# Three gate tiles moved between the last latent heads, and the queries' rotation split between two heads and two engines

## The chip, the cores and the metric

The kernel runs on one core of a Trainium2 chip. Its five engines are TensorE (PE in the profile; its weight loads are PEld), VectorE (DVE), ScalarE (ACT), GpSimd (POOL) and SyncE (SP, which here only issues DMAs; SPq in the profile). The metric is the device time of one execution in microseconds (us), less being better. The profile shows one execution; its times are us from the start of the span.

## The reference

Two transformer blocks follow each other over 512 positions of width 1024: a pooling layer, a multi-head latent attention layer (MLA), a final norm, then a second block with another attention, a spatial gate and a feed-forward part. The change lies in the MLA layer alone:

```python
h = rmsnorm(x, norm_g)
proj = h @ w_in
q_lat, kv_lat, k_rope, z = ...          # 384, 256, 64 and 2048 columns of proj
q = (rmsnorm(q_lat, q_norm_g) @ w_q_b)  # 16 heads of 128 (q_nope) + 64 (q_rope)
kv = (rmsnorm(kv_lat, kv_norm_g) @ w_kv_b)  # 16 heads of 128 (k_nope) + 128 (v)
q_rope, k_rope = apply_rope(...)        # t1*cos - t2*sin, t2*cos + t1*sin
s = (q_nope @ k_nope + q_rope @ k_rope) * scale, causal mask, softmax, @ v
return x + (o.reshape(B, S, 2048) * silu(z)) @ w_out
```

`z` is the gate: 2048 columns, held as 16 chunks of 128.

## The kernel before

All products are made in three passes: each factor is split into a high and a low part, and `three` adds hi*hi, hi*lo and lo*hi in one PSUM bank (eight banks of 128x512). Weights come as tiles of 128x1024 from one stream in HBM. SyncE loads tile t into one of two buffers `raw`, ScalarE makes its high part `w_hi` (`split_tile`, L497), GpSimd its low part `w_lo` (`low_tiles`, L450), TensorE uses it. A ring of four split tiles lies between; `split_tile` for tile t does the work for tile t+3. The order of work on each engine is written out by hand, and each engine goes strictly by its own order: whatever waits holds all behind it on that engine.

**Projection (`mla_in`).** 22 tiles of eight 128-row chunks: 5 latent chunks, one for the key's rotated part, and 16 for the gate. Each is 24 matmuls (`projection`), scaled by `inv` on VectorE into `z` (L1059) and put through Silu on ScalarE (L628). Its input `mla_xg` is written over later by v, q and the rotated queries.

**Heads.** 16 heads in 4 groups (`GROUPS`) of 4 (`GH`). For a group, five weight tiles give 14 units (`GROUP_TILES`): k, q and v of four heads and two rope halves, each half for all four heads. A unit goes to bank 6 or 7; ScalarE copies its high part (L581), VectorE its low part (L999). A group's units are made one group ahead, between the heads of the group before: after head h, `prepare(g, j)` with g = h // 4 + 1 and j = h % 4. With j = 0 come k0 and both rope halves, with j = 1 k1, q0, q1, with j = 2 k2 and q2, with j = 3 k3, q3 and the four v. After heads 12 to 15 there is nothing of this to do.

One head h on TensorE: transposes of its probabilities (L1504), blocks 0 and 1; scores of head h+1 for blocks 0 and 1; transposes and scores for blocks 2 and 3; the product with v (`weigh_mla`); the units. The scores of a block are three products for q and k, two for the rotated part (L1492, L1493) and one of `ident_r` with `mask_r`, which adds the causal mask (L1494). Per head, ScalarE does the high parts of the transposes (L657), the exponentials (L641) and one normalisation (L649); VectorE their low parts (L1118), the maxima (L1099), the normalisation (L1112) and the gate product (L1142). The second pair of transposes waits until VectorE has the low part of block 0.

**Rotation of the queries.** For a group g >= 1 VectorE turns both halves out of the banks with j = 0 (`turn_half`: 2 operations L1010, L1011 for the first half, 4 for the second, L1013 to L1018). With j = 1 ScalarE makes the high parts (`turn_split`, L602) and VectorE the low parts (`turned_low`, L1023). SyncE then places them into `rope_q`: 8 DMAs for the high parts as soon as both are made, 8 for the low (`rope_rows`, L393). SyncE's order is: weight tiles up to the fifth of group g, the 8 high rows, one weight tile, the 8 low rows, four weight tiles. That one weight tile is the one that ScalarE splits with j = 2. The scores of the group's first head, made within head 4g-1 (j = 3), wait for all 16 (`rope_q_in`).

**End of the heads.** ScalarE makes `y_hi` of the finished gate chunks (L556) in heads 12 to 15, GpSimd `y_lo` (L457, 128x512), and `out_product` ("mla_out") uses chunks 0 to 7 with its first tile and 8 to 15 with its second, waiting for each `y_lo`.

Of the kernel before, what the change touches and what calls it, by code (L numbers as in the profile page):

```python
# [21 lines left out]
P = 128  # L22
S = 512
# [28 lines left out]
EPS = 1e-6  # L52
MASKED = -1e30
# [20 lines left out]
TILE_SIZES = (("pool_u", PC), ("pool_z", PC), ("pool_group", PC * PG // 8), ("pool_out", PC), ("mla_in", LC + 1 + PC + 1),  # L74
              ("heads", 5 * GROUPS - 1), ("mla_out", PC), ("mix_qk", 9), ("mix_v", 4), ("mix_z", 8),
# [19 lines left out]

def unit_place(kind, j):
# [8 lines left out]
EARLY = LC + 1 + PC - 3  # L105
# [29 lines left out]
class NormSemaphores:  # L135

    def __init__(self, sem, stage, before, common):
        self.before = before
        self.mean, self.prepared, self.inv = common
        self.x_ready = sem(f"{stage}_x_ready") if stage != "pool" else None  # L140
        self.xg_hi = sem(f"{stage}_xg_hi")
        self.xg_lo = sem(f"{stage}_xg_lo")
        self.squared = sem(f"{stage}_squared")
        self.summed = sem(f"{stage}_summed")
# [15 lines left out]
def build(nc, x_in, stream, columns, counts_in, positions, rows_in, w_s, spill, out):  # L160
# [5 lines left out]
    with ctx:  # L166
# [73 lines left out]
        rope_q = place(112, "rope_q", [P, 2, GH, S], f32r)  # L240
        prob = place(128, "prob", [P, ROW[NB]])
        prob_t_hi, prob_t_lo = (place(133 + 5 * i, f"prob_t_{i}", [P, COLUMN[NB]], f32r) for i in range(2))
        turned_1, turned_2 = place(72, "turned_1", [P, S]), place(74, "turned_2", [P, S])
        rope_t = place(143, "rope_t", [P, S])
# [37 lines left out]
        def col(name, k=0):  # L282
# [11 lines left out]
        common = sem("norm_mean"), sem("norm_prepared"), sem("norm_inv")  # L294
        norm = {n: NormSemaphores(sem, n, before, common)
                for n, before in (("pool", 0), ("mla", 1), ("mix", 2), ("ffn", 4))}
# [18 lines left out]
        x_spilled, x_back = sem("x_spilled"), sem("x_back")  # L315
        unit_done, unit_hi, unit_evac = sem("unit_done"), sem("unit_hi"), sem("unit_evac")
        turned, turned_hi_done, turned_lo_done, rope_q_in = sem("turned"), sem("turned_hi_done"), sem("turned_lo_done"), sem("rope_q_in")

# [39 lines left out]

        def hi_units(u):
# [14 lines left out]
        def _(sp):  # L374
# [20 lines left out]

            for turn, j in sweep(sp, TILE["heads"]):
                load(turn, j)
            for i in range(5 * GROUPS):
# [21 lines left out]
            for turn, j in sweep(sp, TILE["mix_z"] + 3, first=TILE["heads"] + 5 * GROUPS):  # L420
# [15 lines left out]
        def _(pool):  # L436
# [16 lines left out]
            low_tiles(TILE["mla_out"] + RING)  # L453

            for k in range(PC):
# [1391 lines left out]
```

## Time and profile before

| | us |
|---|---|
| median of 3 runs | 1398.18 |
| lowest, highest | 1396.94, 1398.90 |
| the profiled execution | 1397.49 |
| its span | 1395.8 |
| TensorE busy within the span | 1341.2 |

Heads 0 to 15 take from 484.5 to 681.1 us of the span. Projections before and products behind them run with TensorE busy throughout. An idle time in brackets in the timeline is the engine's own, ahead of the row, with what released it; "issue" time has no releaser in the profile. A row's time is from its start to its modelled end, and rows of TensorE overlap.

### The profile page before, as it was taken

What the parts mean: (1) busy time and instruction counts of PE and PEld (TensorE: products, weight loads), DVE (VectorE), ACT (ScalarE), POOL (GpSimd) and SP (SyncE); (2) the same over time, 40 slices, a digit from 0 to 9 for tenths busy, and PEclk for the clock granted to TensorE, in tenths of its full rate; (3) what the DMA queues carried; (4) which work ended last, traced back from release to release, by engine and by line L of the source; (5) the groups of instructions that cost most, each with busy time, mean ns of one, the idle gap of its engine ahead of it and who ended that gap; (6) DMA issues with size and microseconds to landing.
All of it is one profiled execution on the core that took longest, in us unless ns stands there. A gap on an engine that the chain in (4) does not pass through costs nothing.

```text
span 1395.8 us, 16836 instructions
## 1 busy us (share of the span) xinstructions
PE 1341.2 (96%) x6234; PEld 1095.4 (78%) x6234; DVE 656.9 (47%) x1015; ACT 537.9 (39%) x893; POOL 552.2 (40%) x247
## 2 busy tenths in 40 slices
PE   7999999999999999999899999988989999999997
PEld 5888888887788787887788778876768888888886
DVE  7998647133643466666334764466652222221001
ACT  5234333223332555656433335655333223222112
POOL 4446444444353412213544343152344444443441
PEclk9999999999999999999999999999999999999999
DMA  4233222324132421322232336422222223222221
GB/s 153 89 105 119 100 93 91 103 91 151 62 120 78 133 61 46 94 57 77 79 102 91 106 141 177 115 65 95 90 91 90 90 90 97 98 90 91 91 100 67
DMA packets 40589, 135.44 MB, mean 97 GB/s; under 512 B 5937, under 2 KB 5937, under 8 KB 40017
## 3 DMA queue, kind: packets, MB, share of 16 engines
q1 hardware_dynamic: 38800, 126.18, 28.3%
q10 hardware_dynamic: 1728, 8.44, 1.6%
q8 instruction: 40, 0.66, 0.2%
q14 instruction: 21, 0.16, 0.0%
HBM read 117.76 MB, written 6.29 MB: 89 GB/s over the span
## 4 chain that ended last, share of the span: by engine, by line
PE 86%; DVE 5%; ACT 3%; issue 3%; POOL 1%; DMA 1%; SPq 0%; DVEq 0%; ACTq 0%; POOLq 0%
PE bank L1364 27%; PE bank L1366 27%; PE bank L1365 27%; PE bank L1504 2%; PE bank L1492 1%; PE bank L1493 1%; DVE pool_xg L869 1%; ACT f_prob L641 1%; POOL w_lo L450 1%; PE bank L1388 0%; DVE ffn_xg L869 0%; DMA x<-x_in 0%; DVE pool_sqsum L879 0%; ACT w_hi L497 0%; DVE prob_t L1118 0%
## 5 line engine op out<-in xcount | busy, mean ns | idle before, releaser
L450 POOL TENSOR_TENSOR w_lo<-raw,w_hi 128x1024 fp32r<-128x1024 f32 x209 | 513.1, 2456 | 780.1 <-ACT w_hi L497 780.1
L497 ACT ACTIVATE w_hi<-raw 128x1024 fp32r<-128x1024 f32 x209 | 220.2, 1054 | 424.6 <-PE bank L1366 376.9
L1364 PE MATMUL bank<-ffn_xg,w_hi 128*128 128x512 f32 x352 | 140.1, 398 | 5.1 <-DVE ffn_xg L869 5.1
L1366 PE MATMUL bank<-ffn_xg,w_lo 128*128 128x512 f32 x352 | 139.4, 396 | 0.0
L1365 PE MATMUL bank<-ffn_xg,w_hi 128*128 128x512 f32 x352 | 139.4, 396 | 0.0
L1364 PE MATMUL bank<-pool_xg,w_hi 128*128 128x512 f32 x256 | 102.7, 401 | 9.5 <-DVE pool_xg L869 9.5
L1365 PE MATMUL bank<-pool_xg,w_hi 128*128 128x512 f32 x256 | 102.2, 399 | 0.0
L1366 PE MATMUL bank<-pool_xg,w_lo 128*128 128x512 f32 x256 | 102.2, 399 | 0.0
L1364 PE MATMUL bank<-y_hi,w_hi 128*128 128x512 f32 x256 | 101.3, 396 | 0.0
L1366 PE MATMUL bank<-y_hi,w_lo 128*128 128x512 f32 x256 | 101.2, 396 | 0.0
L1365 PE MATMUL bank<-y_lo,w_hi 128*128 128x512 f32 x256 | 101.2, 395 | 0.0
L1364 PEld LDWEIGHTS bank<-ffn_xg,w_hi 128*128 128x128 f32 x352 | 66.1, 188 | 22.8 <-DVE ffn_xg L869 6.6
L1366 PEld LDWEIGHTS bank<-ffn_xg,w_lo 128*128 128x128 f32 x352 | 66.3, 188 | 16.5
L1365 PEld LDWEIGHTS bank<-ffn_xg,w_hi 128*128 128x128 f32 x352 | 66.3, 188 | 16.4 <-issue 0.2
L894 DVE TENSOR_TENSOR x<-bank,x 128x512 f32<-128x512 f32 x16 | 11.1, 692 | 127.8 <-PE bank L1366 127.8
L1364 PE MATMUL bank<-mla_xg,w_hi 128*128 128x512 f32 x176 | 70.2, 399 | 0.0
L1365 PE MATMUL bank<-mla_xg,w_hi 128*128 128x512 f32 x176 | 69.4, 394 | 0.0
L1366 PE MATMUL bank<-mla_xg,w_lo 128*128 128x512 f32 x176 | 69.4, 394 | 0.0
L1366 PE MATMUL bank<-w_hi,act 128*128 128x512 f32 x176 | 69.4, 394 | 0.0
L1364 PE MATMUL bank<-w_hi,act 128*128 128x512 f32 x176 | 69.0, 392 | 0.0
L1365 PE MATMUL bank<-w_lo,act 128*128 128x512 f32 x176 | 69.0, 392 | 0.0
L1364 PEld LDWEIGHTS bank<-pool_xg,w_hi 128*128 128x128 f32 x256 | 48.8, 191 | 21.4 <-POOL w_lo L450 9.5
(333 smaller groups left out, 2845.9 us busy)
## 6 DMA issues: line engine op xcount, KB each, us to landing
raw<-stream SPq DMA_DIRECT2D x209, 512.0 KB, 3.4
spill<-x ACTq DMA_DIRECT2D x2, 2048.0 KB, 6.8
rope_q<-turned_hl SPq DMA_DIRECT2D x64, 64.0 KB, 2.2
stacked<-fq SPq DMA_DIRECT2D x24, 128.0 KB
stacked<-fk SPq DMA_DIRECT2D x24, 128.0 KB
x<-x_in SPq DMA_DIRECT2D x4, 512.0 KB, 6.9
x<-spill ACTq DMA_DIRECT2D x1, 2048.0 KB, 7.7
x<-spill SPq DMA_DIRECT2D x1, 2048.0 KB, 7.8
```

Source lines behind the costliest of these rows:

```text
L450: pool.tensor_tensor(w_lo[:, j % RING, :], raw[:, j % RAW, :], plain(w_hi[:, j % RING, :]), ALU.subtract).then_inc(tile_lo, 1)
L497: act.activation(w_hi[:, t % RING, :], raw[:, t % RAW, :], ACT.Copy).then_inc(tile_hi, 1)
L641: act.activation(target[:, ROW[b]:ROW[b + 1]], bank[SCORE_BANK[b]][:, SCORE_AT[b]:SCORE_AT[b] + n], ACT.Exp, bias=neg_peak[:, h % 2, b:b + ...
L869: dve.scalar_tensor_tensor(xg_lo[:, k, :], x[:, k, :], gain(k), plain(xg_hi[:, k, :]), ALU.mult, ALU.subtract).then_inc(n.xg_lo, 1)
L894: dve.tensor_tensor(x[:, k, :], bank[(k + 4) % 8][:], x[:, k, :], ALU.add).then_inc(n.x_ready, 1)
L1364: pe.matmul(target, a_hi, b_hi, start=start, stop=False)
L1365: pe.matmul(target, a_hi, b_lo, start=False, stop=False)
L1366: return pe.matmul(target, a_lo, b_hi, start=False, stop=stop)
L1492: pe.matmul(target, rope_q[:, g % 2, j, a], rope_k_hi[:, 0:n], start=False, stop=False)
L1493: pe.matmul(target, rope_q[:, g % 2, j, a], rope_k_lo[:, 0:n], start=False, stop=False)
L1504: last = pe.transpose(bank[3 + b % 2][:, P * (q - b):P * (q - b + 1)], source[:, ROW[q] + P * b:ROW[q] + P * (b + 1)], ident[:])
```

## The change

It has three parts. The causal mask as a product on TensorE stands in both kernels alike (L1494 before).

1. **Gate tiles.** The last three gate chunks (`ZN = PC - 3`) leave the projection and get three tiles of their own (`mla_late`) behind the heads' tiles. TensorE makes them after heads 12, 13 and 14 (`late_gate`), in banks 6 and 7, 24 matmuls each. Since their input would be gone, ScalarE stores both parts of `mla_xg` to HBM after the first projection tile (two DMAs of 2 MB), and SyncE reloads them (7 of 8 chunks in three DMAs once group 3's rows are placed, the last chunk after head 11's units). VectorE scales each product, and ScalarE puts it through Silu one head later, with an Exp of one column behind it in head 13.
2. **Rotation.** With j = 0 VectorE turns the first half only; ScalarE copies the second half out of its bank into `rope_2`. VectorE turns it with j = 2, between the normalisation and the gate product. High parts, low parts: with j = 2 instead of j = 1. SyncE's order around the rows is the same.
3. **Order of `y_hi` and `y_lo`.** `y_hi` of chunks 8 and 9 moves from head 14 to head 15. GpSimd takes the four first tiles of `mla_out` between the `y_lo` rather than ahead of them.

```diff
+ZN = PC - 3
+ZX_PARTS = ((108, 3), (143, 3), (72, 1), (64, 1))
...
 sync
+            load(0, TILE["heads"] + 5 * GROUPS)
+            sp.wait_ge(mla.scores, 3 * 12)
+            sp.wait_ge(zx_spilled, 32)
+            sp.wait_ge(rope_q_in, 256 * GROUPS)
+            for i in range(3):
+                reload(i)
+            load(0, TILE["heads"] + 5 * GROUPS + 1)
+            sp.wait_ge(tile_used, group_tile(GROUPS - 1, GH) + 1)
+            reload(3)
...
 gpsimd
-            low_tiles(TILE["mla_out"] + RING)
-            for k in range(PC):
-                pool.wait_ge(y_hi_done, PC + k + 1)
-                pool.tensor_tensor(y_lo[:, k, :], ...)
+            low_tiles(TILE["mla_out"] + 1)
+            first = TILE["mla_out"] + 1
+            for n, chunks in enumerate((range(0, 4), range(4, 8), range(8, 10), range(10, PC))):
+                if n:
+                    low_tiles(first + 1, first=first)
+                    first += 1
+                for k in chunks:
+                    pool.wait_ge(y_hi_done, PC + k + 1)
+                    pool.tensor_tensor(y_lo[:, k, :], ...)
...
 scalar, prepare_tile
+                    elif by_scalar((kind, g, k)):
+                        wait_unit(act, (kind, g, k))
+                        if g > 1:
+                            act.wait_ge(turned, 2 * g)
+                        act.activation(rope_2[:], bank[...][:], ACT.Copy).then_inc(rope_copied, 1)
 scalar, projection
+                if u == 1:
+                    act.wait_ge(norm["mla"].xg_lo, norm["mla"].chunks + DC)
+                    for i, part in enumerate((mla_xg_hi, mla_xg_lo)):
+                        act.dma_start(xg_spill[:, :, i, :], plain(part[:])).then_inc(zx_spilled, 16)
 scalar, heads
                 if g < GROUPS:
-                    if j == 1:
+                    if j == 2:
                         turn_split(g)
                     prepare(g, j)
-                elif h == 12:
+                elif h < HEADS - 1:
+                    split_tile("mla_late", 0, h - 12)
+                else:
                     split_tile("mla_out", 0, 0)
-
-                for k in {12: range(0, 4), 13: range(4, 8), 14: (8, 9), 15: range(10, 14)}.get(h, ()):
+                if h > 12:
+                    n = h - 13 + ZN
+                    act.wait_ge(mla_evac, LC + 1 + n + 1)
+                    act.activation(z[:, n, :], z[:, n, :], ACT.Silu).then_inc(mz_silu, 1)
+                    if h + 2 < HEADS:
+                        settle(act.activation(inv_sum[:, h % 2, 0:1], ones[:, 0:1], ACT.Exp))
+                for k in {12: range(0, 4), 13: range(4, 8), 15: range(8, 14)}.get(h, ()):
                     y_high(k, PC)
...
 vector, heads
+                if j == 0:
+                    unit_low(("k", g, 0))
+                    turn_half(g, 0)
+                    return
...
+                if g < GROUPS and j == 2:
+                    turn_half(g, 1)
                 dve.wait_ge(mla.weighted, h + 1)
                 dve.wait_ge(mz_silu, h + 1)
                 dve.tensor_tensor(z[:, h, :], bank[5][:], z[:, h, :], ALU.mult).then_inc(mla.out, 1)
                 if g < GROUPS:
-                    if j == 1:
+                    prepare(g, j)
+                    if j == 2:
                         turned_low(g)
-                    prepare(g, j)
+                elif h < HEADS - 1:
+                    n = h - 12
+                    dve.wait_ge(tile_used, TILE["mla_late"] + n + 1)
+                    dve.tensor_tensor(z[:, ZN + n, :], bank[6 + n % 2][:], inv[:], ALU.mult).then_inc(mla_evac, 1)
...
 tensor
+            def late_gate(n):
+                wait_tile(0, t)
+                pe.wait_ge(zx_back, 16 * len(ZX_PARTS))
+                ...
+                for k in range(DC):
+                    i, c = ZX_AT[k]
+                    last = three(bank[6 + n % 2][:], *wblock(t, k), zx[i][:, c, 0, :], zx[i][:, c, 1, :], k == 0, k == DC - 1)
...
                 weigh_mla(h)
                 if g < GROUPS:
                     prepare(g, j)
+                elif h < HEADS - 1:
+                    late_gate(h - 12)
```

On ScalarE, this stood between heads 1 and 2 before (`turned_hl`: the high parts of the turned queries; `w_hi`: the split of a weight tile; `prob_t`: the transposes' high parts):

```order
L649 ACTIVATE prob<-prob,inv_sum 128x512
L602 ACTIVATE turned_hl<-turned 128x512 x2
L581 ACTIVATE k<-bank 128x512
L497 ACTIVATE w_hi<-raw 128x1024
L581 ACTIVATE q<-bank 128x512 x2
```

and this stands between heads 2 and 3 now:

```order
L692 ACTIVATE prob<-prob,inv_sum 128x512
L641 ACTIVATE turned_hl<-turned 128x512 x2
L615 ACTIVATE k<-bank 128x512
L530 ACTIVATE w_hi<-raw 128x1024
L615 ACTIVATE q<-bank 128x512
L700 ACTIVATE prob_t<-bank 128x512
```

The pair `turned_hl` moved by one head; the tile split behind it is now that of j = 2.

On SyncE, waits shown, group 1's rows stood and stand alike; this is the kernel after, from the fifth tile of group 1 on:

```order
L398 DMA raw<-stream 128x1024 [waits tile_lo] x5
L409 DMA rope_q<-turned_hl 32x512 [waits turned_hi_done]
L409 DMA rope_q<-turned_hl 32x512 x7
L398 DMA raw<-stream 128x1024 [waits tile_lo]
L409 DMA rope_q<-turned_hl 32x512 [waits turned_lo_done]
L409 DMA rope_q<-turned_hl 32x512 x7
L398 DMA raw<-stream 128x1024 [waits tile_lo] x4
```

Nothing moved here; the two waits now refer to work that stands a head later.

On VectorE the end of head 2 reads now (before, only the last `TENSOR_SCALAR`, `z`, `k` and `q` of these stood there):

```order
L1171 TENSOR_SCALAR prob<-prob,inv_sum 128x384
L1068 TENSOR_TENSOR rope_t<-rope,sin 128x512
L1069 TENSOR_TENSOR turned<-turned,rope_t 128x512
L1071 TENSOR_TENSOR rope_t<-rope,cos 128x512
L1077 TENSOR_TENSOR turned<-turned,rope_t 128x512
L1207 TENSOR_TENSOR z<-bank,z 128x512
L1050 TENSOR_TENSOR k<-bank,k 128x512
L1050 TENSOR_TENSOR q<-bank,q 128x512
L1082 TENSOR_TENSOR turned_hl<-turned,turned_hl 128x512 x2
L1177 TENSOR_TENSOR prob_t<-bank,prob_t 128x512
```

Four operations moved here from the end of head 0, and the two low parts (L1082) from head 1.

## Rows read from the trace of the kernel before

**Rows 1.** The page: busy time, share of the span, instructions.

```profile
PE 1341.2 (96%) x6234; PEld 1095.4 (78%) x6234; DVE 656.9 (47%) x1015; ACT 537.9 (39%) x893; POOL 552.2 (40%) x247
```

**Rows 2.** Waits of TensorE, whole span: us in total, times, longest.

```profile
PE bank L1504 <- DVE prob_t L1118: 8.7, 6, 1.8
```

**Rows 3.** Timeline of VectorE, heads 0 to 2: start, duration, what [idle before].

```profile
497.27 0.69 DVE L1013 TENSOR_TENSOR rope_t<-bank,sin 128x512 f32<-128x512 f32 x1 [0.68 <-PE bank L1366]
...
499.44 0.69 DVE L1018 TENSOR_TENSOR turned<-turned,rope_t 128x512 f32<-128x512 f32 x1
500.06 1.15 DVE L1118 TENSOR_TENSOR prob_t<-bank,prob_t 128x512 fp32r<-128x512 f32 x2
...
507.17 1.28 DVE L1023 TENSOR_TENSOR turned_hl<-turned,turned_hl 128x512 fp32r<-128x512 f32 x2
...
518.47 0.88 DVE L1112 TENSOR_SCALAR prob<-prob,inv_sum 128x128 f32<-128x128 f32 x3
```

**Rows 4.** Timeline of TensorE, heads 0, 1 and 3.

```profile
484.50 0.93 PE L1504 MATMUL bank<-ident,prob 128*128 128x128 f32 x7
...
491.43 0.44 PE L1364 MATMUL bank<-lat,w_hi 128*128 128x512 f32 x1
...
500.89 0.70 PE L1504 MATMUL bank<-ident,prob 128*128 128x128 f32 x3 [1.57 <-DVE prob_t L1118]
...
522.47 0.30 PE L1364 MATMUL bank<-k,q 128*128 128x128 f32 x1
```

**Rows 5.** Timeline of ScalarE, heads 0 to 2.

```profile
491.65 0.72 ACT L649 ACTIVATE prob<-prob,inv_sum 128x512 f32<-128x512 f32 x1 [0.24 <-DVE inv_sum L1109]
...
506.40 1.14 ACT L602 ACTIVATE turned_hl<-turned 128x512 fp32r<-128x512 f32 x2
...
520.38 1.05 ACT L497 ACTIVATE w_hi<-raw 128x1024 fp32r<-128x1024 f32 x1
```

**Rows 6.** SyncE's timeline, group 1: issue start, duration of the series, count.

```profile
507.56 4.95 SPq L393 DMA_DIRECT2D rope_q<-turned_hl  x8
512.55 0.58 SPq L382 DMA_DIRECT2D raw<-stream  x1
513.17 4.94 SPq L393 DMA_DIRECT2D rope_q<-turned_hl  x8
```

**Rows 7.** Landing after issue: tile turned_hl; then line L382, 505 to 530 us.

```profile
DMA to landing us min/median/max: 1.9/2.2/3.8
...
DMA to landing us min/median/max: 3.4/3.7/4.6
```

**Rows 8.** Busy time by window: us, busy (instructions) by engine, clock, DMA share, GB/s.

```profile
345.00:445.00 100.00, 100.00 (x425) 79.24 (x424) 44.49 (x43) 33.51 (x44) 43.10 (x18) 1.00 0.28 90
```

**Rows 9.** Timeline of TensorE, heads 12 to 15.

```profile
647.60 0.93 PE L1504 MATMUL bank<-ident,prob 128*128 128x128 f32 x7
...
676.46 0.98 PE L1504 MATMUL bank<-ident,prob 128*128 128x128 f32 x7 [1.32 <-DVE prob L1112]
...
681.09 0.44 PE L1364 MATMUL bank<-y_hi,w_hi 128*128 128x512 f32 x1
```

**Rows 10.** Timeline of ScalarE: a table load at 120 us, and head 13.

```profile
120.81 1.28 ACT L549 ACT_TABLE_LOAD   x1
122.11 0.63 ACT L549 ACTIVATE z<-z 128x512 f32<-128x512 f32 x1
...
666.78 2.18 ACT L556 ACTIVATE y_hi<-z 128x512 fp32r<-128x512 f32 x4
```

**Rows 11.** Timeline of GpSimd, head 15.

```profile
680.29 7.55 POOL L457 TENSOR_TENSOR y_lo<-z,y_hi 128x512 fp32r<-128x512 f32 x6 [0.95 <-ACT y_hi L556]
```

**Rows 12.** Timeline of TensorE, the first tile: half clock, then full.

```profile
9.51 0.77 PE L1364 MATMUL bank<-pool_xg,w_hi 128*128 128x512 f32 x1 [9.51 <-DVE pool_xg L869]
...
14.77 0.42 PE L1364 MATMUL bank<-pool_xg,w_hi 128*128 128x512 f32 x1
```

**Rows 13.** Landing of the 2 MB transfers (tensor spill), us after issue.

```profile
DMA to landing us min/median/max: 6.3/7.5/7.8
```

More of the change, by code:

```diff
@@ L93 @@
 CHUNKS_OF = {"k": KC, "q": QC, "rope": QC}
+ZX_PARTS = ((108, 3), (143, 3), (72, 1), (64, 1))
+ZX_AT = [(i, c) for i, (_, n) in enumerate(ZX_PARTS) for c in range(n)]
 def unit_place(kind, j):
@@ L240, in build @@
         rope_q = place(112, "rope_q", [P, 2, GH, S], f32r)
+        zx = [place(at, f"zx_{i}", [P, n, 2, S], f32r) for i, (at, n) in enumerate(ZX_PARTS)]
         prob = place(128, "prob", [P, ROW[NB]])
@@ L357, in wait_unit, with by_scalar, evacuated @@
                 engine.wait_ge(unit_done, sum(not ends_tile(o) for o in UNITS[:UNIT[u] + 1]))
+        def by_scalar(u):
+            return u[0] == "rope" and u[1] > 0 and u[2] == 1
+        def evacuated(u):
+            return sum(not by_scalar(o) for o in UNITS[:UNIT[u] + 1])
         def hi_units(u):
@@ L418, in stack_head @@
                     sp.dma_start(slot[at:at + 2, which, :], plain(c_parts[h:h + 1, part:part + 2, :])).then_inc(head_stacked[h % 2], 16)
-            for turn, j in sweep(sp, TILE["mix_z"] + 3, first=TILE["heads"] + 5 * GROUPS):
+            for turn, j in sweep(sp, TILE["mix_z"] + 3, first=TILE["heads"] + 5 * GROUPS + 2):
                 load(turn, j)
@@ L605, in _ @@
             act.dma_start(spill, x[:]).then_inc(x_spilled, 16)
-            for u in range(LC + 1 + PC):
+            for u in range(LC + 1 + ZN):
                 if u == EARLY:
@@ L1030, in prepare_tile @@
                         unit_low((kind, g, k))
-            for u in range(LC + 1 + PC):
+            for u in range(LC + 1 + ZN):
                 if u == EARLY:
@@ L1373, in wait_tile, with projection @@
                 pe.wait_ge(tile_lo, turn * RING + (t + 1))
-            def projection(stage, turn, j, b, xg_hi, xg_lo, xg_lo_done=None):
+            def projection(stage, turn, j, b, xg_hi, xg_lo, first=None):
                 t = TILE[stage] + j
@@ L1379, in projection @@
                 for k in range(DC):
-                    if xg_lo_done is not None:
-                        pe.wait_ge(xg_lo_done, k + 1)
+                    if first is not None:
+                        pe.wait_ge(first.xg_lo, first.chunks + k + 1)
                     last = three(b[:], *wblock(t, k), xg_hi[:, k, :], xg_lo[:, k, :], k == 0, k == DC - 1)
@@ L1406, in _ @@
                     pe.wait_ge(in_evac, turn * RING + (j - 3))
-                projection("pool_u", turn, j, bank[j % 4], pool_xg_hi, pool_xg_lo, n.xg_lo if starts(turn, j, 1) else None)
+                projection("pool_u", turn, j, bank[j % 4], pool_xg_hi, pool_xg_lo, n if starts(turn, j, 1) else None)
                 if starts(turn, j, 2) and j == 1:
@@ L1460, in _ @@
             n = norm["mla"]
-            for u in range(LC + 1 + PC):
+            for u in range(LC + 1 + ZN):
                 if u < 4:
@@ L1704, in _ @@
                     pe.wait_ge(ffn_evac, turn * RING + (j - 3))
-                projection("ffn_up", turn, j, bank[j % 4], ffn_xg_hi, ffn_xg_lo, n.xg_lo if starts(turn, j, 1) else None)
+                projection("ffn_up", turn, j, bank[j % 4], ffn_xg_hi, ffn_xg_lo, n if starts(turn, j, 1) else None)
                 if starts(turn, j, 1):
```

83 lines of the change are left out of this document (52 added, 31 removed).

## The prediction

> **What bounds the kernel now.** I read the page's busy times first: TensorE is busy for 1341.2 of 1395.8 us [rows 1], so it is the bound and all that can be won or lost is its idle time and its half-clock time. Next come TensorE's waits: 8.7 us in six waits for `prob_t`'s low part [rows 2]. The timeline of the heads shows where. At the end of heads 0, 4 and 8 VectorE turns both rope halves, its last operation starts at 499.44, and the low part that TensorE needs follows at 500.06 [rows 3]; TensorE stood still 1.57 us for it at 500.89 [rows 4]. There are three of these, 4.7 us. The rest lies in heads 13 to 15, where TensorE has no units to make and each head goes at the pace of the chain of transposes, copies, maxima and exponentials: from 647.60 to the first `mla_out` product at 681.09 [rows 9], 33.5 us. A head with nothing to wait for takes 6.9 us (484.50 to 491.43) [rows 4]. The last view is SyncE's timeline, because the change moves the source of its rows but not the rows: group 1's 8 high rows are issued from 507.56, one weight tile at 512.55, the 8 low rows from 513.17 for 4.94 us [rows 6]. So the last row is issued at about 517.5 and landed 2.2 us later [rows 7], at 519.7. The scores that need it began at 522.47 [rows 4]. The slack there is 2.8 us, and the change takes away more than a head.
>
> **Gate tiles: a gain.** One tile is 24 matmuls; the projection runs 425 in 100 us [rows 8], so 5.6 us a tile, 16.8 us for three, which leave the projection. Before, these plus heads 12 to 15 took 16.8 + 33.5 = 50.3 us. Now: three heads of 6.9, three tiles of 5.6, and head 15 as before (676.46 to 681.09, 4.6 us) [rows 9], together 42.2. That is 8.1 us won, if nothing on the other engines is late. Two things are.
> ScalarE in head 13 has, after its normalisation, a tile split (1.05), a table load, Silu, a second table load, Exp and four `y_hi`. A table load takes 1.28 and the next operation starts 1.30 after it; four `y_hi` take 2.18, so 0.54 each [rows 5, 10]. The normalisation ends 0.9 after TensorE starts its filler (492.37 against 491.43) [rows 4, 5]. The sum is 0.9 + 1.0 + 1.3 + 0.6 + 1.3 + 0.3 + 2.2 = 7.6 us, against 5.6 for the gate tile and 0.7 until the first transposes can be copied: 1.3 us late, and TensorE with it. Head 12 (0.9 + 1.0 + 2.2) and head 14 (one table load, no `y_hi`: 3.8) hide under the tile.
> GpSimd at the end: six `y_lo` took 7.55 us before, 1.25 each [rows 11], and a tile's low part 2.4 (43.10 us for 18) [rows 8]. From 0.8 us behind the end of head 15 it has chunks 8 and 9, then the low part of a tile, then chunks 10 to 15, ready at 13.2 us. TensorE uses chunks 8 to 15 from 5.6 us on, 0.7 each, to 11.2. It gets chunk 11 at 8.2 and then goes at GpSimd's pace: 2.8 us lost. Before, GpSimd was done early enough.
> Net gain of this part: 8.1 - 1.3 - 2.8 = 4.0 us; bounds 0 (half clock during both stalls) and 8.1.
> On table loads the Trainium skill, page "ScalarE: Activation LUTs", section "What ACT_TABLE_LOAD costs", gives 1.28 us for the load and another 1.38 us of drain for each change of set. This trace has the 1.28, but Silu started 1.30 us after the load began and no drain is seen behind it [rows 10]. By the page's figure head 13 would come 2.8 us later still, and the total would be 1457.5.
>
> **Rotation at j = 0: a gain.** VectorE does two operations there instead of six, and ScalarE's copy of 0.6 us falls into its idle time. The three waits of 1.57 us go: 4.7 us. Next late would be the low part's ordinary wait of 0.2 us, which a free head has inside its 6.9.
>
> **Rotation at j = 2: the large loss.** I follow group 1 with before's times for head 2. VectorE's normalisation runs from 518.47 for 0.88, to 519.35. The four turns took 497.27 to 500.13, 2.86 us [rows 3]: done at 522.2. ScalarE then makes both high parts, 1.14 [rows 5]: 523.4. Only now may SyncE issue the 8 high rows, 4.95 us, and behind them, in the same queue, the weight tile: issued at 528.4 [rows 6], landed 3.4 to 3.7 us later [rows 7], 532.0. ScalarE in head 2 needs exactly this tile: its split stood at 520.38 before [rows 5]. It now runs to 533.0. Behind it on ScalarE stand q2's high part (0.55), and the high parts of head 3's transposes. VectorE waits for q2 (0.7, to 534.2), since `turned_low` stands behind it (1.28 [rows 3], to 535.5). Then the 8 low rows: the last is issued 4.3 us later and lands after another 2.2, at 542.0. TensorE, which stands at the scores of head 4 since 522.47, waits 19.5 us. Its own work behind the wait needs nothing else that is late: the transposes' high and low parts were done meanwhile, so little is gained back. The same orders stand in groups 2 and 3: 3 x 19.5 = 58.5 us. Bounds: 17 to 21 a group, by the landing times' spread (1.9 to 3.8, 3.4 to 4.6) [rows 7].
> After a wait TensorE starts at half clock, 1.2 GHz. The only idle time of this length before is the 9.51 us at the start: from 9.51 to 14.77 it did 12 matmuls in 5.3 us instead of 2.8 [rows 12], a row every 0.43 us against 0.233. I take 2.3 us a group, 6.9 together; bounds 0 and 2.6 each.
>
> **Storing and reloading `mla_xg`.** 4 MB are written during the projection. A 2 MB transfer landed in at most 7.8 us [rows 13], while DMAs moved 90 GB/s with a share of 0.28 in that stage [rows 8], and a weight tile is used three tiles after its split. I take 0; bound 3 us. The reload of 3.7 MB waits for group 3's rows, so it starts when TensorE starts head 11's rest. At 2 MB in 7.8 us it is through about 13 us later, with a weight tile behind it that ScalarE needs about 12 to 14 us after that start, by before's pace plus the half clock: 0.5 us; bounds 0 and 5. The last chunk has head 12 as its cover.
>
> **The sum.** Against the profiled execution of 1397.5 us: + 58.5 + 6.9 + 0.5 - 4.7 - 4.0 = + 57.2, so 1454.7. That execution lies 0.7 below the median. Forecast: **1455 us**, 4% slower. The mask's product is in both kernels and adds nothing.
>
> **Rivals.**
> *The rows come late, but ScalarE does not wait for the tile.* If the tile were there in time, q2's high part would end at 525.5, and the low rows would follow the high ones at 529.0: last landing at 535.5, 13.0 us a group, total 1435. For it: VectorE and ScalarE alone would be fast enough. Against it: the tile stands behind the 8 rows in SyncE's order, with `raw` of two buffers.
> *Transfers collide.* If the reload's seven chunks of 512 KB land one by one at 3.7 us [rows 7], it takes 26 us instead of 13, and the units of head 11 and the first gate tile wait for it: 13 us more, 1468. For it: they are the largest transfers in one place. Against: 2 MB came in 7.8 us.
> *The rows are not late and the kernel is faster.* Without the stall and its half clock, 1397.5 + 0.5 - 4.7 - 4.0 = 1389.3. This holds only if the chain from 519.35 to 542.0, 22.7 us, takes 3.1 us or less. The 16 row issues alone are 9.9 us, so it needs rows issued from elsewhere or needed later than I read.
> *The parts do not do what they are for.* If the gate tiles win nothing because ScalarE and GpSimd hold the end, 1459; that lies in the forecast's range.
>
> **How the numbers follow.** Chances: forecast 0.82, first rival 0.07, collision 0.06, faster 0.04, and 0.01 for ending within 0.2% of before, which is about what a measurement of this kernel can tell from no change. The range of the main case by its bounds: three stalls of 17 to 21, half clock, end and reload give about 1445 to 1468; the upper end takes in most of the collision case and I set the lower end at 1441, since two landings shorter than their medians would add up over three groups. Faster 0.04, same 0.01, slower 0.95.
>
> **What would show each step.** In the profile after: TensorE's waits must show three idle times of about 19 us in heads 3, 7 and 11, with a scores matmul or a DMA into `rope_q` at their end; SyncE's timeline the high rows a head later, the tile right behind, the low rows some 7 us after the tile; ScalarE a wait of about 8 us for `raw` in heads 2, 6, 10; the 1.57 us waits gone; heads 12 to 15 at about 12.5 us each with a late second transpose only in head 14; TensorE short stops within the second `mla_out` tile. I am wrong if the rows land before the scores, if the wait is under 10 us, or if the projection gains idle time while `mla_xg` is stored.

## The result, and the profile after

| | before | after |
|---|---|---|
| median of 4 runs, us | 1398.04 | 1452.00 |
| lowest, highest | 1396.94, 1398.90 | 1451.09, 1457.00 |
| profiled execution, its span | 1397.49, 1395.8 | 1451.43, 1449.7 |

The changed kernel is slower: ratio 1.0394, 95% interval 1.0369 to 1.0419. The forecast was 1455.0 with a range of 1441 to 1468. Between the two profiled executions lie 53.9 us.

The page of the changed kernel has TensorE busy for as long as before (1341.3 for 1341.2 us [rows 1]), so the whole difference of the two spans is idle time: 108.4 us for 54.6. Matmuls at half clock count as busy. Those behind the new stalls took longer, but others that ran at half clock before did not do so here, and the two cancel (see "Half clock" and the table of stretches below). The clock line shows three dips in the middle, one for each stall:

```profile
PE 1341.3 (93%) x6234; PEld 1096.0 (76%) x6234; DVE 659.9 (46%) x1015; ACT 543.8 (38%) x900; POOL 552.7 (38%) x247
...
PEclk9999999999999979797999999999989999999999
```

TensorE's waits in the changed kernel (line, what for: us in total, times, longest):

```profile
PE bank L1433 <- issue: 61.8, 3, 20.8
...
PE bank L1575 <- DVE prob_t L1177: 2.3, 2, 1.2
...
PE bank L1433 <- POOL y_lo L491: 1.3, 5, 0.3
```

The first line is new and holds the loss. "issue" only says that the profile found no instruction that released TensorE; what did has to be read from the other engines. The second line answers to the 8.7 us in six waits of [rows 2]: the three of 1.57 us are gone, and of the three in heads 13 to 15 two are left.

The timelines of the changed kernel in heads 2 and 3 (start, duration, engine, line, what, count, idle before) show the chain of group 1, from VectorE's last turn at 501.09 to TensorE at 522.88. In this order: VectorE, ScalarE, SyncE.

```profile
501.09 0.69 DVE L1077 TENSOR_TENSOR turned<-turned,rope_t 128x512 f32<-128x512 f32 x1
...
513.32 0.69 DVE L1050 TENSOR_TENSOR q<-bank,q 128x512 fp32r<-128x512 f32 x1 [9.14 <-ACT q L615]
513.93 2.45 DVE L1082 TENSOR_TENSOR turned_hl<-turned,turned_hl 128x512 fp32r<-128x512 f32 x2
```

```profile
501.82 1.15 ACT L641 ACTIVATE turned_hl<-turned 128x512 fp32r<-128x512 f32 x2 [2.98 <-DVE turned L1077]
...
511.75 1.06 ACT L530 ACTIVATE w_hi<-raw 128x1024 fp32r<-128x1024 f32 x1 [8.29 <-DMA raw<-stream]
512.71 0.58 ACT L615 ACTIVATE q<-bank 128x512 fp32r<-128x512 f32 x1
```

```profile
503.00 4.95 SPq L409 DMA_DIRECT2D rope_q<-turned_hl  x8
507.99 0.58 SPq L398 DMA_DIRECT2D raw<-stream  x1
516.40 4.94 SPq L409 DMA_DIRECT2D rope_q<-turned_hl  x8
```

TensorE in the same place, then in heads 7 and 11 (timeline):

```profile
501.44 0.93 PE L1575 MATMUL bank<-ident,prob 128*128 128x128 f32 x7
522.88 0.45 PE L1433 MATMUL bank<-k,q 128*128 128x128 f32 x1 [20.52 <-issue]
...
597.60 0.45 PE L1433 MATMUL bank<-k,q 128*128 128x128 f32 x1 [20.77 <-issue]
...
672.20 0.44 PE L1433 MATMUL bank<-k,q 128*128 128x128 f32 x1 [20.47 <-issue]
```

So the weight tile is issued behind the eight high rows at 507.99, ScalarE gets it at 511.75 after 8.29 us of waiting, q2's high part comes behind it, VectorE has waited 9.14 us for that, and the low parts and the eight low rows (last issue about 520.7) follow. Landings of the rows took 2.0 us in the median, which gives 522.7; TensorE goes on at 522.88.

### The profile page after: what moved, and what is told of

It reads as the page before. It is cut to its first block, busy times and chain, and to the rows that moved or that the text cites. A ratio compares the mean times of both kernels' runs of the same rounds, so it can differ in the third digit from the quotient of the medians.

```text
span 1449.7 us, 16847 instructions
## 1 busy us (share of the span) xinstructions
PE 1341.3 (93%) x6234; PEld 1096.0 (76%) x6234; DVE 659.9 (46%) x1015; ACT 543.8 (38%) x900; POOL 552.7 (38%) x247
## 4 chain that ended last, share of the span: by engine, by line
PE 81%; DVE 5%; issue 4%; ACT 4%; DMA 3%; POOL 2%; SPq 2%; DVEq 0%; ACTq 0%; POOLq 0%
PE bank L1433 26%; PE bank L1435 25%; PE bank L1434 25%; DMA raw<-stream 2%; PE bank L1575 2%; SPq L409 1%; POOL y_lo L491 1%; PE bank L1563 1%; PE bank L1564 1%; POOL w_lo L480 1%; DVE pool_xg L920 1%; ACT f_prob L684 1%; ACT w_hi L530 1%; PE bank L1457 0%; DVE ffn_xg L920 0%
## 5 line engine op out<-in xcount | busy, mean ns | idle before, releaser
L1433 PE MATMUL bank<-k,q 128*128 128x128 f32 (+1 forms) x64 | 25.8, 402 | 63.2 <-issue 61.8
L1434 PEld LDWEIGHTS bank<-ffn_xg,w_hi 128*128 128x128 f32 x352 | 66.4, 189 | 16.6 <-issue 0.5
L1433 PEld LDWEIGHTS bank<-k,q 128*128 128x128 f32 x64 | 13.4, 209 | 64.2 <-issue 62.4
L1433 PE MATMUL bank<-mla_xg,w_hi 128*128 128x512 f32 x152 | 60.9, 401 | 0.0
```

The lines of the kernel that those rows point to most:

```text
L1433: pe.matmul(target, a_hi, b_hi, start=start, stop=False)
L1434: pe.matmul(target, a_hi, b_lo, start=False, stop=False)
```

## The experiments

Eight kernels were timed beside the kernel before, whose median was 1397.9 to 1398.0 in each set. "After" is the changed kernel. Ratios are to before.

**1. Each half alone.** Is the loss the rotation's, and are the two halves independent? The first kernel undoes the rotation in after and keeps the gate tiles.

```diff
-            return u[0] == "rope" and u[1] > 0 and u[2] == 1
+            return False
...
-                    if j == 2:
+                    if j == 1:
                         turn_split(g)
...
-                if j == 0:
-                    unit_low(("k", g, 0))
-                    turn_half(g, 0)
-                    return
...
-                if g < GROUPS and j == 2:
-                    turn_half(g, 1)
...
-                    prepare(g, j)
-                    if j == 2:
+                    if j == 1:
                         turned_low(g)
+                    prepare(g, j)
```

> The kernel after with the rotation put back as it was: VectorE turns both halves with j = 0, high and low parts with j = 1; gate tiles and the new order of y_lo stay. Theory (the loss is the rows of the rotated queries, placed a head later): the stalls at heads 3, 7 and 11 are gone, the 1.57 us waits at heads 0, 4, 8 are back, and the rest of the change measured by stretches (18.6 us less before head 0, 9.7 more from head 12 to the first mla_out product, 2.6 more in the two first mla_out tiles, 1.4 less behind) gives about 1390.5 us. Rival (storing and reloading mla_xg, or the new end, costs more than it seems): over 1400 us.

Measured: 1391.99 us (1390.99 to 1395.76), ratio 0.9953, interval 0.9940 to 0.9967: 6 us less than before, where 7.4 were expected. The rotation's waits are back (7.0 us in five waits for `prob_t`'s low part).

The second puts the rotation part alone into before (ScalarE's copy `rope_2`, the second half turned, split and placed with j = 2); the gate tiles stay in the projection.

```diff
+                        act.activation(rope_2[:], bank[UNIT_BANK[UNIT[(kind, g, k)]]][:], ACT.Copy).then_inc(rope_copied, 1)
...
-                    if j == 1:
+                    if j == 2:
                         turn_split(g)
...
+                if g < GROUPS and j == 2:
+                    turn_half(g, 1)
...
-                    if j == 1:
-                        turned_low(g)
                     prepare(g, j)
+                    if j == 2:
+                        turned_low(g)
```

> The kernel before with the rotation's part of the change alone: ScalarE copies the second half, VectorE turns it with j = 2, high and low parts with j = 2. No gate tile is moved. Theory: heads 0 to 12 take 61 us more as in the full change, so about 1459 us, with three idle times of TensorE of 20 us. Rival (the stalls need the reload or the late tiles beside them): near 1398 us, or clearly less than 1459.

Measured: 1458.26 us (1457.26 to 1461.03), ratio 1.0431, interval 1.0417 to 1.0445. TensorE's waits have the same line as after's:

```profile
PE bank L1392 <- issue: 61.7, 3, 20.7
```

The rotation costs 60.3 us by itself and the gate tiles give 6.0. The sum, 1452.3, is within the scatter of the changed kernel's 1452.0: these runs show no effect of one half on the other.

**2. Is the queue's order the cause?** In the forecast's chain the eight row issues stand twice, once ahead of the tile that ScalarE waits for and once ahead of the scores. The rival was that the chain of VectorE, ScalarE and the rows is long enough by itself. Here SyncE loads the one tile ahead of the high rows; nothing else is moved.

```diff
             for i in range(5 * GROUPS):
-                load(0, TILE["heads"] + i)
+                if i < 9 or (i - 4) % 5:
+                    load(0, TILE["heads"] + i)
+                if i >= 8 and (i - 3) % 5 == 0:
+                    load(0, TILE["heads"] + i + 1)
```

> The kernel after with one thing moved: in SyncE's order the weight tile that stood between the 8 high and the 8 low rows now stands ahead of the high rows. Theory (ScalarE waits for this tile, behind the rows, and with it q2's high part, VectorE's turned low parts and the low rows): ScalarE's 8.3 us wait for raw goes, the low rows are issued from about 508.1 instead of 516.4 us of the span in group 1, and each stall falls from 20.5 to about 12.3 us: 1427 us. Rival (the turning a head later alone sets the time, whatever stands in the queue): 1452 us.

Measured: 1429.55 us (1429.39 to 1430.57), ratio 1.0226, interval 1.0211 to 1.0242. SyncE's, TensorE's and ScalarE's timeline:

```profile
502.99 10.01 SPq L409 DMA_DIRECT2D rope_q<-turned_hl  x16
```

```profile
514.54 0.45 PE L1436 MATMUL bank<-k,q 128*128 128x128 f32 x1 [12.17 <-issue]
```

```profile
503.35 1.04 ACT L533 ACTIVATE w_hi<-raw 128x1024 fp32r<-128x1024 f32 x1
```

ScalarE waits for nothing, the 16 rows go out in one series, and the stall shrinks from 20.6 to 12.3 (means of three). So the tile's place in the queue costs 8.3 us a group, and 12.3 stay because 10.0 us of row issues begin at 503, after TensorE has come to the scores at 502.4. The price that the first rival named for this case was 13.0. Whether rows issued from a second queue would shorten the 12.3 was not tried.

The time is 2.6 us above the 1427 expected. Between the profiled executions of after and of this kernel the stalls shrink by 25.0 us in all, and heads 0 to 12 by 23.5 (224.6 to 201.1). From head 15's first transposes to the end, where the two kernels have the same code, it takes 722.1 us for 720.6 (on this scatter see the last section).

**3. The same from the other end.** SyncE's order stays, and VectorE makes the turned low parts ahead of q2's, so that the low rows don't depend on the late tile.

```diff
                 if g < GROUPS:
-                    prepare(g, j)
                     if j == 2:
                         turned_low(g)
+                    prepare(g, j)
```

> The kernel after with one thing moved on VectorE: the low parts of the turned queries stand ahead of k2's and q2's low parts, so they do not wait for ScalarE's tile split. The tile still stands between the rows. Theory: the low rows are bounded by SyncE alone, 4.95 us of high rows, 0.6 for the tile, then the low rows: first issue near 508.6 instead of 516.4, each stall about 7.8 us shorter, 1429 us. ScalarE still waits for the tile. Rival (VectorE's order does not matter because ScalarE's wait holds TensorE anyway): 1452 us, or a stall that ends with ScalarE's high parts of the transposes.

Measured: 1432.55 us (1431.71 to 1434.21), ratio 1.0244, interval 1.0228 to 1.0259. SyncE's, ScalarE's and TensorE's timeline:

```profile
507.85 0.58 SPq L398 DMA_DIRECT2D raw<-stream  x1
508.47 4.94 SPq L409 DMA_DIRECT2D rope_q<-turned_hl  x8
```

```profile
512.51 1.06 ACT L530 ACTIVATE w_hi<-raw 128x1024 fp32r<-128x1024 f32 x1 [9.19 <-DMA raw<-stream]
```

```profile
514.96 0.45 PE L1433 MATMUL bank<-k,q 128*128 128x128 f32 x1 [12.73 <-DVE q L1050]
```

The low rows now follow the tile at once, although ScalarE still waits 9.19 us for it. So the rival, by which ScalarE's wait holds TensorE anyway, fell. TensorE's wait is put down to q2's low part, which ended 0.17 us before it went on. But these scores, head 4's, need q0's and not q2's, and the rows fit better: in after, here and in experiment 2, TensorE went on 2.13 us after the last row's issue began (issues of 0.59 at the end of the three series: 520.75 to 522.88, 512.83 to 514.96, 512.41 to 514.54). So the name in the wait is that of a neighbour. The stalls are 12.8 us each (38.5 of the 39.9 us for that releaser in the list of waits, the fourth wait being one of 1.4 us ahead of head 0's scores), 0.56 more than in experiment 2, which is the tile's own issue between the two series.

The stalls are 7.8 us shorter than in after, as expected, and yet the time is 3.5 us above the 1429 expected. Between the profiled executions of after and of this kernel heads 0 to 12 shrink by 21.5 us for 23.3 of stalls. From head 15's first transposes to the end, with the same code, it takes 725.0 us for 720.6, which is scatter and no cost of the edit. Against experiment 2 the heads take 2.0 us more, of which the tile's issue makes 1.7. Experiments 2 and 3 agree on the cause: the 8.3 us are the tile between the two series and the low rows behind the tile's work. Either order undone takes them away. What is left, 12.3 us, goes with the 16 issues in series (10.0) and the last landing, which begin when TensorE is already there.

**4. Rows that start earlier.** The second half is turned, split and placed with j = 1, and only ScalarE's copy is kept from the change's rotation. The rows then go out as early as before.

```diff
-                    if j == 2:
+                    if j == 1:
                         turn_split(g)
...
-                if g < GROUPS and j == 2:
+                if g < GROUPS and j == 1:
                     turn_half(g, 1)
...
-                    prepare(g, j)
-                    if j == 2:
+                    if j == 1:
                         turned_low(g)
+                    prepare(g, j)
```

> The kernel after with the rotation's later steps one head earlier: VectorE turns the second half with j = 1, ahead of the gate product, and high and low parts are made with j = 1, the low parts ahead of k1's. ScalarE's copy into rope_2 stays. Theory (it is the head in which the rows are issued that costs): the high rows are issued near 490.6 us of the span in group 1, the last low row lands near 502.6, where the scores wait from about 502.4: at most 1 us is left of each 20.5 us stall. New: k1's low part comes about 3 us later, and q1's product needs its bank, so a wait of 1.5 to 3 us in heads 1, 5, 9. Total 1390 to 1396 us. Rival (the copy and the two halves apart cost by themselves): over 1405 us.

Measured: 1398.21 us (1396.08 to 1403.13, 11 runs), ratio 1.0002, interval 0.9993 to 1.0010: the same as before. All of the stalls are gone, but the four turns at the end of head 1 hold up k1's low part, and TensorE waits for its bank. TensorE's waits and its timeline:

```profile
PE bank L1433 <- DVE k L1050: 8.5, 3, 2.8
```

```profile
493.33 0.50 PE L1433 MATMUL bank<-lat,w_hi 128*128 128x512 f32 x1 [2.83 <-DVE k L1050]
```

I expected 1390 to 1396. Against the gate tiles alone it loses 6.2: 8.5 us of new waits for 4.7 us of old ones makes 3.8. In this kernel's profiled execution the third of the three waits, at 603.88, had half clock behind it (0.83 granted from 602 to 612) and the first two had none (1.00): head 9 took 16.6 us for 15.6 of heads 1 and 5. So half clock can make 1.0 of the remaining 2.4 in a run; the rest stays open.

**5. The small waits at the end.** From the gate tiles alone, GpSimd makes all the low parts of chunks 8 to 15 ahead of the fourth `mla_out` tile's low part.

```diff
-            for n, chunks in enumerate((range(0, 4), range(4, 8), range(8, 10), range(10, PC))):
+            for n, chunks in enumerate((range(0, 4), range(4, 8), range(8, PC))):
```

> The kernel of the gate tiles alone (rotation as before the change) with one more edit on GpSimd: the fourth mla_out tile's low part stands behind y_lo of chunks 8 to 15 instead of behind chunk 9. Theory (GpSimd's 2.4 us tile in the middle of the y_lo costs 2.6 us in the second mla_out tile): y_lo 15 is ready 2.4 us earlier, and the time falls by 2 to 2.6 us, to 1389.7. Rival (TensorE loses there for another reason, or the tile's low part is late for its own use): 1392 us or more.

Measured: 1390.91 us (1390.65 to 1391.03), ratio 0.9951, interval 0.9938 to 0.9963. The waits for `y_lo` are gone. Against the gate tiles alone it is 1.1 us less, where 2.3 were expected; the two kernels' runs overlap, so no gain is shown in the time. The traces show it in its place: ScalarE's seventh split of a weight tile behind the start of head 15 begins 38.85 us after it, and 41.10 with the gate tiles alone (707.11 from 668.26, 709.96 from 668.86), so 2.25 us were won there. Of the waits left in TensorE's timeline two belong to the gate tiles, one in head 11 and the one forecast for head 14, with `y_hi` in head 13 as its cause:

```profile
628.08 0.50 PE L1427 MATMUL bank<-w_hi,lat 128*128 128x512 f32 x1 [1.79 <-DVE v L1050]
...
657.95 0.70 PE L1569 MATMUL bank<-ident,prob 128*128 128x128 f32 x3 [1.03 <-DVE prob_t L1177]
```

The next kernel also takes `y_hi` of chunks 6 and 7 out of head 13, and GpSimd's order follows (the third tile's low part stands behind chunk 5).

```diff
-                for k in {12: range(0, 4), 13: range(4, 8), 15: range(8, 14)}.get(h, ()):
+                for k in {12: range(0, 4), 13: (4, 5), 14: (6, 7), 15: range(8, 14)}.get(h, ()):
```

> As the kernel before it, and ScalarE makes y_hi of chunks 6 and 7 in head 14 instead of head 13 (GpSimd's order follows). Theory (ScalarE in head 13, with two table loads and four y_hi, is 1.3 us late for head 14's transposes, and two y_hi are 1.1 us): the 1.0 us wait of head 14 goes, 1388.7 us. Rival (drain behind each table load, by which ScalarE would be 4 us late): under 0.5 us gained, the wait stays over 2 us.

Measured: 1390.08 us (1387.28 to 1393.19), ratio 0.9944, interval 0.9932 to 0.9956. The head-14 wait is gone. So `y_hi` in head 13 was its cause. The time was expected at 1388.7, and the 0.8 us won are less than these runs can tell apart.

**6. The copy with a better cover.** Last, ScalarE's copy with the second half turned inside the head with j = 1, two operations behind each pair of low parts of the transposes, rather than in one piece.

```diff
                 transposed_low(mla, h, prob_t_hi, prob_t_lo, (0, 1))
+                if g < GROUPS and j == 1:
+                    turn_second(g, 0)
...
                 transposed_low(mla, h, prob_t_hi, prob_t_lo, (2, 3))
+                if g < GROUPS and j == 1:
+                    turn_second(g, 1)
...
                     if j == 1:
+                        unit_low(("k", g, 1))
                         turned_low(g)
-                    prepare(g, j)
+                        unit_low(("q", g, 0))
+                        unit_low(("q", g, 1))
+                    else:
+                        prepare(g, j)
```

> As the kernel before it, with the idea of the rotation's change moved to where rows are in time: ScalarE copies the second half with j = 0; VectorE turns it in head j = 1, two operations behind the transposes' low parts of blocks 0 and 1, two behind those of blocks 2 and 3; high and low parts with j = 1, k1's low part ahead of the turned low parts. Theory: the 1.57 us waits at heads 0, 4, 8 and the half clock behind one of them go (6 us), while maxima and normalisation come 1.5 to 2.9 us later where 4.4 us are free, and k1's low part 1 to 2 us late for q1's bank: a net gain of 1 to 4 us, 1386 us. Rival (the gain is given back whole in q1's wait): 1389 us or more.

Measured: 1390.74 us (1387.77 to 1392.25), ratio 0.9949, interval 0.9937 to 0.9962. The 1.57 us waits are gone. The 1386 expected were missed, and the rival's "1389 us or more" came. In the place of those waits, TensorE's waits and its timeline:

```profile
PE bank L1450 <- DVE k L1050: 4.5, 3, 1.5
PE bank L1592 <- DVE prob_t L1188: 3.7, 4, 1.2
```

```profile
490.44 0.50 PE L1450 MATMUL bank<-lat,w_hi 128*128 128x512 f32 x1 [1.52 <-DVE k L1050]
...
495.73 0.70 PE L1592 MATMUL bank<-ident,prob 128*128 128x128 f32 x3 [0.83 <-DVE prob_t L1188]
```

So 4.7 us of waits went, and 4.5 for k1's bank and three of 0.83 for the transposes of head 2 and its like came: 7.0 in all, though the medians differ by 0.7 only, which is less than the runs tell apart. The turns push k1's low part back, and the turned low parts push back those of q0 and q1. Where VectorE's work for the rotation stands within the head decides who waits, not whether. The gate tiles alone and the three kernels of experiments 5 and 6 have medians of 1390.1 to 1392.0, better than both before and after; they can't be told from one another.

## Why the prediction was right

**The chain, step by step.** The forecast followed group 1 in before's times. In after, VectorE's normalisation of head 2 starts at 498.12 where it started at 518.47 [rows 3], so 20.35 is taken off each:

| step | forecast | less 20.35 | measured |
|---|---|---|---|
| last turn done | 522.2 | 501.85 | 501.78 |
| first high row issued | 523.4 | 503.05 | 503.00 |
| tile issued | 528.4 | 508.05 | 507.99 |
| tile there, split begins | 532.0 | 511.65 | 511.75 |
| q2's low part done | 534.2 | 513.85 | 514.01 |
| turned low parts done | 535.5 | 515.15 | 516.38 |
| last low row landed, TensorE goes on | 542.0 | 521.65 | 522.88 |

All steps but one hold within 0.2 us. The one that failed, a size and not the mechanism, is the price of the two turned low parts: 1.28 us, from a row of before in which VectorE was alone [rows 3]; here they took 2.45. GpSimd shows why (timeline of after):

```profile
512.88 2.35 POOL L480 TENSOR_TENSOR w_lo<-raw,w_hi 128x1024 fp32r<-128x1024 f32 x1 [21.88 <-ACT w_hi L530]
```

The late tile releases GpSimd's low part too, and it runs from 512.88 to 515.23, over the start of the turned low parts at 513.93. In experiment 2 the same pair took 2.44 beside that operation; in experiment 3, where GpSimd was idle, it took 1.29. So the stalls were 1.0 to 1.3 us longer than forecast (20.5 to 20.8 for 19.5), 61.8 us in all for 58.5.

**Half clock.** Forecast 2.3 us a group. The windows of after (us, busy with counts of PE, PEld, DVE, ACT, POOL, granted clock, DMA share, GB/s), right behind the first stall:

```profile
522.00:528.00 6.00, 5.12 (x23) 5.11 (x24) 1.68 (x6) 1.36 (x6) 0.00 (x0) 0.57 0.53 185
```

A mean of 0.57 over 6 us is 5.2 us at the lower level, 1.2 GHz; 0.9 of these lie ahead of 522.88, so 4.3 us of work were done at half speed: 2.1 us lost, within 0.2 of the forecast. By the lengths of heads 3, 7 and 11 (38.95, 39.37 and 39.72 us for 16.62, 16.62 and 16.61), less the waits, it is 1.8, 2.0 and 2.2: 6.0 us for the 6.9 forecast.

The forecast left out that before had half clock in the heads as well. Of its three waits of 1.57 us the third, at 608.71, had it behind, the first had not (windows of before, columns as above):

```profile
606.00:616.00 10.00, 8.44 (x43) 7.50 (x43) 7.03 (x19) 4.39 (x14) 0.00 (x0) 0.83 0.01 2
497.00:507.00 10.00, 8.43 (x54) 7.45 (x53) 8.02 (x20) 5.14 (x15) 0.10 (x1) 1.00 0.01 2
```

Head 9 took 15.63 us there, heads 1 and 5 14.24. So what the rotation won was not 4.7 us but 6.7: 1.8, 1.8 and 3.2.

**Gate tiles.** Forecast 4.0 us won. From the start of head 12's transposes to the first `mla_out` product it was 43.5 us, of which 1.3 for a late head 14. After's timeline of TensorE:

```profile
690.53 0.93 PE L1575 MATMUL bank<-ident,prob 128*128 128x128 f32 x7
...
718.85 0.70 PE L1575 MATMUL bank<-ident,prob 128*128 128x128 f32 x3 [1.04 <-DVE prob_t L1177]
...
733.74 0.45 PE L1433 MATMUL bank<-y_hi,w_hi 128*128 128x512 f32 x1
```

That is 43.2, and the late head is 14, by 1.04; head 15 takes 4.6 us as before. The 33.5 us that this replaces had half clock in them (granted clock 0.95; 3.4 us of it behind a wait of 1.84 in head 13), the 43.2 have none (1.00), so 1.7 of the 8.1 us won are clock. ScalarE's timeline in head 13 holds the table load as costed, 1.30 us from its start to the next operation:

```profile
713.78 1.28 ACT L727 ACT_TABLE_LOAD   x1
715.07 0.20 ACT L727 ACTIVATE inv_sum<-ones 128x1 f32<-128x1 f32 x1
715.30 2.19 ACT L589 ACTIVATE y_hi<-z 128x512 fp32r<-128x512 f32 x4
```

No drain stands behind it. As an estimate by the figure of the Trainium skill, page "ScalarE: Activation LUTs", section "What ACT_TABLE_LOAD costs" (another 1.38 us of drain behind the load), the next operation would start at 716.4; it started at 715.07, and the measurement decides.

In the second `mla_out` tile the forecast was 2.8 us lost to GpSimd, from chunk 11 on. GpSimd's and TensorE's timeline in after:

```profile
736.90 2.41 POOL L480 TENSOR_TENSOR w_lo<-raw,w_hi 128x1024 fp32r<-128x1024 f32 x1
739.24 7.52 POOL L491 TENSOR_TENSOR y_lo<-z,y_hi 128x512 fp32r<-128x512 f32 x6
```

```profile
741.86 0.50 PE L1433 MATMUL bank<-y_hi,w_hi 128*128 128x512 f32 x1 [0.22 <-POOL y_lo L491]
...
746.82 0.50 PE L1433 MATMUL bank<-y_hi,w_hi 128*128 128x512 f32 x1 [0.27 <-POOL y_lo L491]
```

A chunk every 1.24 us in place of 0.70, five times, is 2.7; the 1.3 us in the list of waits are only half of it. The rest is that the row ahead of each wait and the row behind it no longer overlap, and that the first matmul is slower (0.50 for 0.39). The release of this tile's buffer comes 14.1 us after the first product, against 11.5 before: 2.6.

**The old waits and the reload.** The three waits of 1.57 us are gone: head 1 takes 12.46 us in after (478.51 to 490.97), where it took 14.24. The reload's 0.5 us is one wait in head 11:

```profile
689.03 0.50 PE L1433 MATMUL bank<-w_hi,lat 128*128 128x512 f32 x1 [0.43 <-DVE v L1050]
```

The other kernels with the gate tiles have this wait at nothing to 1.8 us, within the forecast's bounds of 0 and 5.

Storing `mla_xg` costs nothing in the projection (window of after, us and busy as above):

```profile
327.00:440.00 113.00, 113.00 (x479) 89.80 (x478) 55.76 (x54) 38.60 (x51) 45.20 (x19) 1.00 0.43 148
```

TensorE is busy for all of it, with DMAs at a share of 0.43.

**Where the missing 3.3 us lie.** By stretches of the two profiled executions:

| stretch | forecast | measured |
|---|---|---|
| start to head 0's transposes | -16.8 | -18.6 |
| head 0's transposes to head 12's | +61.2 | +61.5 |
| head 12's to first `mla_out` product | +10.0 | +9.7 |
| first two `mla_out` tiles | +2.8 | +2.6 |
| behind them | 0 | -1.4 |
| sum | +57.2 | +53.9 |

(61.2 is 58.5 + 6.9 + 0.5 - 4.7. The third line is 42.2 + 1.3 - 33.5.) That the second line comes out within 0.3 is luck in part: stalls 3.3 us too short stand against half clock 0.9 too long in heads 3, 7 and 11 and 2.0 too little won in heads 1, 5 and 9, 1.4 of it half clock of before. The rest is 1.8 us ahead of the heads and 1.4 behind the second tile. Of the first, 1.5 are head 0's first scores (10.81 us from 473.69 to 484.50, and 9.29 from 456.63 to 465.92), which ran at half clock in before's execution and at full in after's. Windows of before, of after, and of the gate tiles alone over the same work:

```profile
470.00:485.00 15.00, 13.59 (x63) 11.21 (x62) 6.89 (x17) 9.22 (x18) 4.85 (x3) 0.89 0.22 72
```

```profile
450.00:466.00 16.00, 14.59 (x72) 11.84 (x71) 7.75 (x18) 10.71 (x20) 6.09 (x3) 1.00 0.28 98
```

```profile
450.00:466.00 16.00, 14.59 (x65) 11.88 (x63) 6.86 (x16) 9.57 (x18) 4.76 (x2) 0.89 0.30 98
```

The kernel with the gate tiles alone does the same work in the same places as after up to there and has the half clock, so it is no part of the change. The 1.4 us behind the second tile are no waits: those add up to 22.8 us in before and 23.2 in after, but the same 3160 matmuls keep TensorE busy for 672.4 us in before and 670.5 in after. One place where the clock differs lies over the same work in the second block (before, then after):

```profile
855.00:875.00 20.00, 18.26 (x132) 17.32 (x131) 8.36 (x29) 10.85 (x28) 4.79 (x2) 0.91 0.53 142
```

```profile
908.00:928.00 20.00, 18.26 (x145) 17.59 (x145) 8.11 (x29) 10.82 (x28) 5.41 (x3) 1.00 0.57 147
```

So of the missing 3.3 us most is clock at two places where the change did nothing, and the errors in its steps nearly cancel.

**The range.** Added up at their ends, the bounds of the prediction's terms give 1436 to 1472, not "about 1445 to 1468". The measured 1452.0 lies well inside both.

**The rivals.** "ScalarE does not wait for the tile" was made true in experiment 2, which priced it: 12.3 us a group for 13.0. "Transfers collide" fell with the reload's 0.4 us. "The rows are not late" needed the chain to take 3.1 us; it took 23.9 (499.0 to 522.9), where 22.7 were forecast. "The parts do not do what they are for" fell with experiment 1: the gate tiles give 6.0 us, where the forecast had 4.0. By the stretches they give 18.6 - 9.7 - 2.6 = 6.3 in after, of which 1.5 are head 0's clock.

## What to carry over

Before a step is moved later, follow every instruction it issues into its queue: here eight row DMAs moved one head later stood ahead of a weight tile, and that tile stood ahead of the very work which the next rows needed, and 4.7 us of waits won came back as 20.6 us three times. When such a loop is cut, ask what the rows in series still cost by themselves: 12.3 us of each stall stayed, until the rows started a head earlier. Make the halves of a change separately: one of these two was worth 6 us and was hidden under 60. And compare a forecast term by term: this one came within 0.3 us over the heads with three terms off by 1 to 3 us.

## What the runs showed of the hardware

**VectorE's operations from SBUF to SBUF waited for GpSimd's.** Two operations with both inputs in SBUF took 1.29 us while GpSimd was idle, 2.44 and 2.45 us where its `w_lo` was running when they began, and 3.48 us in the last kernel, where `w_lo` began while the first of the two ran. Its VectorE and GpSimd timeline:

```profile
490.31 3.48 DVE L1093 TENSOR_TENSOR turned_hl<-turned,turned_hl 128x512 fp32r<-128x512 f32 x2
```

```profile
490.69 2.54 POOL L480 TENSOR_TENSOR w_lo<-raw,w_hi 128x1024 fp32r<-128x1024 f32 x1 [12.26 <-ACT w_hi L530]
```

In all three cases the held operation (1.84, 1.85 and 2.88 us, where one is 0.68 alone) ends 0.54 to 0.56 us after GpSimd's does (506.82, 515.23 and 493.23), as if it had done its work only then; q2's low part, with one input in PSUM, kept its 0.69 beside the same `w_lo`. The Trainium skill, page "SBUF — State Buffer", section "Who interferes with whom", says that a VectorE instruction with two SBUF inputs contends with a GpSimd instruction that reads SBUF; it calls the port pair that they share an exclusive lock and says that the order of issue decides who is held. These rows agree.

**A wait of a given length does not decide the clock.** All ten profiled executions have TensorE idle for 1.41 us ahead of head 0's scores; three of them (before, the gate tiles alone, experiment 4) are at half clock, 1.2 GHz, behind it, the others are not. Of the three waits of 1.57 us in before and of the three of 2.83 us in experiment 4, the third alone has half clock behind it. Behind each of the twelve stalls of 12 us and more it was at 1.2 GHz.

**Kernels differed where their code is the same.** Runs of one kernel were 0.4 to 7.1 us apart. From head 15's first transposes to the end, after and the kernels of experiments 1 (gate tiles), 2, 3 and 4 have the same code, and their profiled executions took 720.6, 725.1, 722.1, 725.0 and 724.4 us. Behind the first 25 us of that stretch the same 3133 matmuls kept TensorE busy for 664.2 to 668.0 us. That is why gains of 1 us could not be shown in the time of a run here, only in their place in a trace.
